# First attention of a two-block transformer kernel: mask and maximum in one VectorE instruction, row sums divided out by diagonal matrices on TensorE, w_ada blocks moved under the rotations

## The reference

```python
# differential head
s1 = q1 @ k1.T * scale;  s2 = q2 @ k2.T * scale        # 256 x 256, causal, 128-query blocks
p1 = softmax(where(mask, s1, -inf));  p2 = softmax(where(mask, s2, -inf))
out = (p1 - lam * p2) @ v
# indexed sparse head: the 64 keys per query with the highest index score, shared by the eight heads
score = sum_h iw[t, h] * relu(iq[t, h] . ik[s]);  sel = top_k(score, 64)
out = softmax(where(valid, q @ k_sel.T * scale, -inf)) @ v_sel
# modulation of the block, from the conditioning vector
mod = silu(c) @ w_ada + b_ada                          # w_ada is 2048 x 12288
```

## Time and profile before

| what | us |
|---|---|
| median of 3 runs | 2853.45 (2843.34 to 2854.09) |
| the profiled execution's own time | 2851.65 |
| its span, first to last instruction | 2849.9 |
| rotations | 354 to 383 |
| index scores | 388 to 410 |
| heads of the first attention | 411 to 491 |

### The profile page before, as it was taken

One profiled execution on the slowest core, in us unless ns is written; L12 is line 12 of the kernel. 1 busy time (PEld: TensorE's weight loads), 2 busy tenths in 40 slices (PEclk: granted clock), 3 DMA queues, 4 the chain that ended last, 5 costly groups with the idle time before them and its releaser, 6 DMA issues. The chain is left out here.

```text
span 2849.9 us, 48016 instructions
## 1 busy us (share of the span) xinstructions
PE 2627.3 (92%) x20028; PEld 2396.6 (84%) x20028; DVE 1424.9 (50%) x1857; ACT 1047.5 (37%) x1335; POOL 268.4 (9%) x324
## 2 busy tenths in 40 slices
PE   5999977969999999999879979798899999999998
PEld 3888834959999999999859947348899999999998
DVE  2455577856674444343353354524555555554443
ACT  3533225334334343333233325323244444443333
POOL 4000030230000000011122000101200000000000
PEclk8999999989999999999989979768999999999999
DMA  7777747745776555555535411002455555554553
GB/s 281 258 247 275 266 146 278 280 138 185 260 271 210 181 189 178 166 190 185 177 89 177 147 37 60 30 0 97 149 169 177 178 178 189 177 182 159 189 182 112
DMA packets 260588, 501.54 MB, mean 176 GB/s; under 512 B 16160, under 2 KB 23035, under 8 KB 260219
## 3 DMA queue, kind: packets, MB, share of 16 engines
q1 hardware_dynamic: 249888, 492.99, 51.5%
q10 hardware_dynamic: 10603, 7.18, 0.9%
HBM read 498.05 MB, written 2.10 MB: 175 GB/s over the span
## 5 line engine op out<-in xcount | busy, mean ns | idle before, releaser
L1127 DVE TENSOR_TENSOR w_lo<-raw,w_hi 128x2048 fp32r<-128x2048 f32 (+2 forms) x386 | 861.1, 2231 | 1079.0 <-ACT w_hi L735 1078.9
L1657 PE MATMUL bank<-x_hi,w_hi 128*128 128x256 f32 (+3 forms) x4608 | 1313.0, 285 | 54.2 <-DVE w_lo L1127 19.2
L1658 PE MATMUL bank<-x_lo,w_hi 128*128 128x256 f32 (+3 forms) x4608 | 1309.8, 284 | 0.0
L1659 PE MATMUL bank<-x_hi,w_lo 128*128 128x256 f32 (+3 forms) x4608 | 1307.8, 284 | 0.0
L735 ACT ACTIVATE w_hi<-raw 128x2048 fp32r<-128x2048 f32 (+2 forms) x386 | 719.1, 1864 | 1075.6 <-PE bank L1659 925.1
L1657 PEld LDWEIGHTS bank<-x_hi,w_hi 128*128 128x128 f32 (+1 forms) x4608 | 875.5, 190 | 90.3 <-issue 40.5
L1659 PEld LDWEIGHTS bank<-x_hi,w_lo 128*128 128x128 f32 (+1 forms) x4608 | 876.6, 190 | 0.0
L1658 PEld LDWEIGHTS bank<-x_lo,w_hi 128*128 128x128 f32 (+1 forms) x4608 | 872.6, 189 | 0.0
L1657 PE MATMUL bank<-hid_hi,w_hi 128*128 128x256 f32 x1408 | 400.0, 284 | 7.9 <-POOL hid_lo L646 6.6
L1658 PE MATMUL bank<-hid_lo,w_hi 128*128 128x256 f32 x1408 | 399.0, 283 | 0.0
L1659 PE MATMUL bank<-hid_hi,w_lo 128*128 128x256 f32 x1408 | 398.9, 283 | 0.0
(11 more groups left out here) (259 smaller groups left out, 1547.3 us busy)
## 6 DMA issues: line engine op xcount, KB each, us to landing
raw<-in_w_ada SPq DMA_DIRECT2D x88, 1024.0 KB, 5.3
raw<-in_w_gate SPq DMA_DIRECT2D x88, 1024.0 KB, 5.2
raw<-in_w_up SPq DMA_DIRECT2D x88, 1024.0 KB, 5.2
raw<-in_w_in SPq DMA_DIRECT2D x68, 1024.0 KB, 5.5
raw<-in_w_down SPq DMA_DIRECT2D x64, 1024.0 KB, 5.1
raw<-in_w_down SPq DMA_DIRECT2D x32, 768.0 KB, 4.3
raw<-in_w_o SPq DMA_DIRECT2D x16, 1024.0 KB, 6.5
raw<-in_w_out SPq DMA_DIRECT2D x16, 1024.0 KB, 5.1
```

The costliest lines, as they stand in the source:

```text
L1127: dve.tensor_tensor(w_lo[ps][:, 0:width], raw[slot][:, 0:width], w_hi[ps][:, 0:width], ALU.subtract).then_inc(raw_free[slot], 1)
L1657: pe.matmul(out, wh[:, k, c], hi(k0 + k), start=a0, stop=False)
L1658: pe.matmul(out, wh[:, k, c], lo(k0 + k), start=False, stop=False)
L1659: ins = pe.matmul(out, wl_[:, k, c], hi(k0 + k), start=False, stop=z)
```

## The change

What it does:

- For heads 0 to 15, `mask` is one `tensor_tensor_reduce` per segment: (scores + bias) times -scale, written to the sheet, with the minimum (the negated maximum) as its accumulated output. The exponential takes scale -1.
- `normalise` only inverts the row sums. GpSimd makes diagonal matrices `diag` (identity times inverse row sum, for sheet 1 also times -lambda), four per differential head and two per dsa head (`diagonals`). `turn` multiplies each sheet block with its matrix, both sheets accumulating in the bank, in place of the transposes.
- The turned dsa sheet is copied by VectorE (`take_turned`) instead of ScalarE.
- Blocks 10 and 11 of w_ada go under the rotations, 12 and 13 between the index scores, 14 to 16 between the heads, one quarter per head and the columns after each fifth head.
- `scores(g)` no longer waits for `h_exp` for g below 26; `exps(g)` also waits for `h_normed` of head g - 2, which GpSimd now sets.

```diff
@@ -267,6 +267,7 @@
         pool_note = place("pool_note", [1, 8])
         gpad_at = cursor[0]
         gpad = place("gpad", [P, 4, NC])
+        diag = place("diag", [P, 2, 4, P], at=gpad_at)
         rope2 = place("rope2", [64, 2, N2], at=gpad_at)
         turns2 = place("turns2", [64, N2], at=gpad_at + 8 * N2)
         acc_at = cursor[0]
@@ -342,6 +343,7 @@
                 i_scored, i_relu, i_added, selected = (sem("index_scored"), sem("index_relu"), sem("index_added"),
                                                sem("selected"))
+        h_inverse = sem("head_inverse")
         h_scored, h_masked, h_exp, h_normed, h_turned, h_copied, h_out, h_taken, h_low = (
             sem("head_" + s) for s in ("scored", "masked", "exp", "normed", "turned", "copied", "out", "taken", "low"))
         m_query, m_scored, m_masked, m_exp, m_normed, m_turned, m_copied, m_out, m_taken = (
@@ -685,6 +687,22 @@
                 pool.wait_ge(bank_freed, BLOCKS_IN1 * 4 + 4)
                 pool.wait_ge(rope_ready, 4)
             rotate_cos("one", projected1)
+
+            def diagonals(g):
+
+                s = g % 2
+                pool.wait_ge(h_inverse, g + 1)
+                if g >= 2:
+                    pool.wait_ge(h_turned, g - 1)
+                for j in range(4 if kind(g) == "diff" else 2):
+                    inv = total[:, s, j:j + 1]
+                    if j < 2:
+                        ins = pool.tensor_scalar(diag[:, s, j, :], ident, inv, None, ALU.mult)
+                    else:
+                        ins = pool.tensor_scalar(diag[:, s, j, :], ident, inv, lamv[:, 5:6], ALU.mult, ALU.mult)
+                ins.then_inc(h_normed, 1)
+            for g in range(16):
+                diagonals(g)
             pool.wait_ge(tile_done, 4 + 4 * BLOCKS_IN1 + 1)
             presum_start("attn_post")
             presum_blocks("attn_post", branch_a, BLOCKS_IN1)
@@ -885,18 +903,24 @@
                     act.activation(lamv[:, 2:4], lamv[:, 0:2], ACT.Exp).then_inc(lam_exp, 1)
                     sines(0, [rope1[:, k, :] for k in range(4)])
 
+            for s in (ADA_HEADS, ADA_HEADS + 1):
+                take_row(s)
+                take_columns(s)
+
             for h in range(16):
                 act.wait_ge(i_scored, h + 1)
                 if h >= 2:
                     act.wait_ge(i_added, h - 1)
                 act.activation(relu[:, h % 2, :], bank[h % 4][:, 0:3 * P], ACT.Relu).then_inc(i_relu, 1)
                 if h in (3, 11):
-                    take_row(ADA_HEADS + h // 8)
+                    take_row(ADA_HEADS + 2 + h // 8)
                 elif h in (7, 15):
-                    take_columns(ADA_HEADS + h // 8)
+                    take_columns(ADA_HEADS + 2 + h // 8)
 
             def exps(g):
                 act.wait_ge(h_masked, g + 1)
+                if 2 <= g < 18:
+                    act.wait_ge(h_normed, g - 1)
                 s = g % 2
                 n = SEGS[kind(g)]
                 for j, (sheet, c0, c1) in enumerate(n):
@@ -907,11 +931,13 @@
                     else:
                         sh = (sheets if g < 16 else sheets2)[:, g % 3, sheet, c0:c1]
                         ins = act.activation(sh, sh, ACT.Exp, bias=peak[:, s, j:j + 1],
-                                             accum_out=total[:, s, j:j + 1])
+                                             scale=-1.0 if g < 16 else 1.0, accum_out=total[:, s, j:j + 1])
                 ins.then_inc(h_exp, 1)
 
             def copy_turned(g):
                 s = g % 2
+                if kind(g) == "dsa":
+                    return
                 act.wait_ge(h_turned, g + 1)
                 if g >= 2:
                     act.wait_ge(h_out, g - 1)
@@ -935,10 +961,10 @@
                 for g in range(g0, g1):
                     if g + 1 < g1:
                         exps(g + 1)
-                    if g < 16 and g % 3 == 2:
-                        take_row(ADA_HEADS + 2 + g // 3)
-                    if g < 16 and g % 3 == 0 and g:
-                        take_columns(ADA_HEADS + 1 + g // 3)
+                    if g < 15 and g % 5 == 4:
+                        take_row(ADA_HEADS + 4 + g // 5)
+                    if g in (5, 10, 15):
+                        take_columns(ADA_HEADS + 3 + g // 5)
                     copy_turned(g)
                     if g > g0:
                         take_out(g - 1)
@@ -1370,13 +1396,15 @@
                     dve.wait_ge(h_turned, g - 2)
                 segs = SEGS[what]
                 sh = (sheets if g < 16 else sheets2)[:, g % 3]
-                if what == "diff":
-                    chain(*[dve.scalar_tensor_tensor(sh[:, m, :], bank[4 * s + m][:, 0:3 * P], QK_SCALE1,
-                                                     causal[:, :], ALU.mult, ALU.add) for m in range(2)])
-                elif what == "dsa":
-                    chain(dve.scalar_tensor_tensor(sh[:, 0, :], bank[4 * s][:, 0:3 * P], DSA_SCALE, selbias[:, :],
-                                                   ALU.mult, ALU.add))
-                elif what == "na":
+                if g < 16:
+                    hidden, scale = (causal, QK_SCALE1) if what == "diff" else (selbias, DSA_SCALE)
+                    for j, (sheet, c0, c1) in enumerate(segs):
+                        ins = dve.tensor_tensor_reduce(sh[:, sheet, c0:c1], bank[4 * s + sheet][:, c0:c1],
+                                                       hidden[:, c0:c1], -scale, -NEG, ALU.add, ALU.min,
+                                                       peak[:, s, j:j + 1])
+                    ins.then_inc(h_masked, 1)
+                    return
+                if what == "na":
                     links = []
                     for b in range(2):
                         rows = bias_na[:, h, 2 - 2 * b:6 - 2 * b, :].rearrange("p r c -> p (r c)")
@@ -1397,19 +1425,23 @@
                 segs = SEGS[what]
                 sh = (sheets if g < 16 else sheets2)[:, g % 3]
                 tot = total[:, s]
+                if g < 16:
+                    dve.reciprocal(tot[:, 0:len(segs)], tot[:, 0:len(segs)]).then_inc(h_inverse, 1)
+                    return
                 chain(dve.reciprocal(tot[:, 0:len(segs)], tot[:, 0:len(segs)]))
-                if what == "diff":
-                    chain(dve.tensor_scalar(tot[:, 2:4], tot[:, 2:4], lamv[:, 5:6], None, ALU.mult),
-                          *[dve.tensor_scalar(sh[:, 0, c0:c1], sh[:, 0, c0:c1], tot[:, j:j + 1], None, ALU.mult)
-                            for j, (_, c0, c1) in enumerate(segs[0:2])])
-                    for j, (_, c0, c1) in enumerate(segs[0:2]):
-                        ins = dve.scalar_tensor_tensor(sh[:, 0, c0:c1], sh[:, 1, c0:c1], tot[:, 2 + j:3 + j],
-                                                       sh[:, 0, c0:c1], ALU.mult, ALU.add)
-                else:
-                    for j, (sheet, c0, c1) in enumerate(segs):
-                        ins = dve.tensor_scalar(sh[:, sheet, c0:c1], sh[:, sheet, c0:c1], tot[:, j:j + 1], None,
-                                                ALU.mult)
+                for j, (sheet, c0, c1) in enumerate(segs):
+                    ins = dve.tensor_scalar(sh[:, sheet, c0:c1], sh[:, sheet, c0:c1], tot[:, j:j + 1], None,
+                                            ALU.mult)
                 ins.then_inc(h_normed, 1)
+
+            def take_turned(g):
+                if kind(g) != "dsa":
+                    return
+                s = g % 2
+                dve.wait_ge(h_copied, g)
+                dve.wait_ge(h_turned, g + 1)
+                dve.wait_ge(h_out, g - 1)
+                dve.tensor_copy(turned[:, s, 0:3 * P], bank[4 * s + 2][:, 0:3 * P]).then_inc(h_copied, 1)
 
             def take_low(g):
                 if kind(g) != "dsa":
@@ -1427,8 +1459,11 @@
                     normalise(g)
                     if g < 7:
                         topk_beside(g)
+                    if g > g0:
+                        take_turned(g - 1)
                     if g > g0 + 1:
                         take_low(g - 2)
+                take_turned(g1 - 1)
                 take_low(g1 - 2)
                 take_low(g1 - 1)
             heads(0, 16)
@@ -1822,6 +1857,10 @@
                         ins = pe.matmul(out, idn, flat(rope_at(rope_buf(which, 1, src), r, src)), start=False,
                                         stop=True)
                     ins.then_inc(r_sum, 1)
+                    if which == "one" and j % 8 in (1, 2, 3, 4) and j < 16:
+                        ada_quarter(ADA_HEADS + j // 8, j % 8 - 1)
+                    elif which == "one" and j % 8 == 7:
+                        ada_columns(ADA_HEADS + j // 8)
             rotate("one")
 
             def turn_values(first, tiles, meta):
@@ -1851,16 +1890,17 @@
                 pe.matmul(b[:, 0:P], q[:, 0:P], ikk[r, 0:P], start=True, stop=True)
```

(20 more changed lines are left out.)

## The result

The changed kernel took 2830.58 us (median of 8 runs, 2828.05 to 2839.73) beside 2852.45 of before (8 runs); the ratio is 0.9933, 95% interval 0.9917 to 0.9950.

A forecast was written before the change was run, and what follows sets the result against it. VectorE was taken to bound the differential heads and TensorE the dsa heads. Differential heads -9.6, dsa heads -1.0 and rotations +1.4 gave -9.2 us, from 2853.45 to 2844 us, with 2834 to 2855 as the 8-in-10 range.

The forecast's parts named there:

- the sum: Whole kernel: differential heads -9.6, dsa heads -1.0 and rotations +1.4 make -9.2 us.
- M = 2.0: VectorE's mask in a differential head: four fused instructions and four readouts take 2.0 us, bounds 1.4 to 3.0.
- The period of 4.1: Differential heads: one head takes 4.1 us after the change, from the loop between the engines.
- my own ring: Differential heads: scores, mask, reciprocal, matrices, turn, outputs, quarter and hand-overs form a loop of two periods, 4.1 us each.
- D = 2.0: GpSimd's four matrices of a differential head, at 0.6 and 0.35 us each with hand-overs: 2.0 us, bounds 1.3 to 2.7.
- The rivals about GpSimd: Heads: GpSimd becomes the bound, 2849 us (chance 0.13); GpSimd is shut out while VectorE works, 2893 us (chance 0.04).
- the second one: Differential heads: GpSimd becomes the bound, 0.85 us per matrix, 3.4 per head, period 4.8, time 2849 us; chance 0.13.
- The half clock at the first turn: Differential heads: first turn, quarter and scores of head 3 run at half clock, making VectorE wait some 2 us.
- dsa heads -1.0: dsa heads: TensorE's work per head becomes 3.56 us, the eight together 31.5 instead of 32.5, so -1.0 us.
- Rotations +1.4: Rotations: quarters cost nothing at full clock, but the first meets a low clock, so +1.4 us (0.3 to 4).
- The median lies 1.8 above it: 2853.45 - 9.2: Whole kernel: the median lies 1.8 us above the profiled execution, so 2853.45 less 9.2 gives 2844 us.
- Only VectorE's work counts: Rival: readouts overlap, matrices take 1.3, TensorE keeps its clock; differential heads -13.5, dsa -2, rotations +0.5: 2838.5 us; chance 0.20.

The follow-up runs named there:

- e8: The changed kernel with the first two diagonal matrices of every head made twice on GpSimd, with a hand-over between; 2847.9 us.
- e10: The changed kernel with dsa heads the old way (normalised on VectorE, transposed, copied on ScalarE); 2835.6 us, turn of head 7 to turn of head 15 25.57.
- e5: The kernel before with only the relaxed wait (scores of heads 2 to 25 no longer wait for the exponentials); 2847.4 us.
- e1: The kernel before with only the fused mask (exponential with scale -1); 2840.9 us.
- e2: The kernel before with only the w_ada blocks moved; 2852.4 us.
- e13: The kernel before with the fused mask and the moved w_ada blocks, without the matrices; 2841.0 us.
- e12: The kernel before with eight tiny chained VectorE instructions ahead of the statistics of the second attention's last heads; 2844.2 us.
- e7: The changed kernel with eight tiny chained VectorE instructions ahead of the statistics of the second attention's last heads; 2830.6 us.
- e11: The changed kernel with dsa heads the old way and the w_ada quarters two rotation steps later; 2825.5 us.
- e14: A repeat of e11, the changed kernel with dsa heads the old way and later w_ada quarters; 2828.8 us.
- e9: The changed kernel with the eight w_ada quarters under rotation steps 3 to 6 and 10 to 13, columns after steps 9 and 16; 2832.4 us.
- e4: The changed kernel with the wait of the scores for the exponentials put back for heads 2 to 25; 2836.6 us.
- e3: The changed kernel with the w_ada blocks back where they were before; 2844.4 us.

## Why the prediction was wrong

The number was off by 13.4 us (2844 and 2830.6), and the heads are not where it was lost: there the sum said -9.2 and the traces have -9.55. From one profiled execution to the other the forecast was -9.2, and they differ by 20.7. What is missing is 3.3 us between `out1` and 644 and 8 us in the long stretch at half clock, both behind the part that the forecast walked through; it put all of that at nothing. Two steps failed, the level of the runs (the bullet on the median; it put the time outside the range) and the price of the mask (the first bullet; the sum hides it).

- **The mask, M = 2.0, bounds 1.4 to 3.0: the step of the mechanism that failed.** It is 1.12. The fused instruction's price was right (0.28 and 0.42 forecast, 0.285 and 0.421 measured), and the readout's too (0.08). Wrong was "I take 2.0, near the upper end, since a readout has to wait for what it reads": its row stands beside that of the next instruction and holds nothing up. The bound of 1.4 was too high as well: "overlapped" still charged the readouts in part. By the rule of the Trainium skill, VectorE: DVE Perf Modes (Rules for kernel authors), not to fuse for speed, the mask would gain nothing here; the measured one, seven instructions to eight and 2.30 us to 1.12, speaks against counting instructions in this case.
- **The period of 4.1 was right for a wrong reason.** By my own ring with M = 1.12 it would be (0.76 + 1.12 + 0.15 + 2.05 + 1.44 + 0.75 + 0.99 + 0.4) / 2 = 3.8. The period is 4.05 because TensorE's own work is 4.05, where I had 3.7: turn 1.44 for 1.3, quarter 0.99 for 0.88, scores 0.87 for 0.76. Two errors, in M and in TensorE's sum, cancelled in the period and not at the start: the reciprocal of head 0 came 3.13 after the first mask in place of 4.3. Differential heads -11.45 for -9.6.
- **D = 2.0** was right: 2.05, of 0.600 and 0.441 for 0.6 and 0.35. The rivals about GpSimd were rightly held unlikely. e8 made the case of the second one real, D of about 3.4: it said 41.8 us from the first mask to the turn of head 7, and 40.04 were measured.
- **The half clock at the first turn** was right: the clock was 0.50 from 417.6 to 424.4, TensorE's scores came late and VectorE waited 4.41 us once, where I had 2.
- **dsa heads -1.0:** to the last copy 32.96 became 32.76, -0.2. A head takes 3.64 for 3.56, and 0.4 more comes behind the last turn. C of e10, 2.42 us shorter, shows that the old turn was the better one here.
- **Rotations +1.4, with "nothing" for a quarter at full clock:** +2.5. A step with a quarter takes 2.05 us, not 1.68, since a pair of rotation matmuls occupies 1.06 and a quarter 0.99, back to back:

```profile
360.45 1.06 PE L1727 MATMUL bank<-raw,csilu 128*32 128x512 f32 x8
361.44 1.12 PE L1853 MATMUL bank<-rope_s,cst 128*128 128x512 f32 x2
362.50 1.06 PE L1727 MATMUL bank<-raw,csilu 128*32 128x512 f32 x8
```

  I had 0.86 + 0.88 = 1.74 from rows of other shapes and wrote off 0.1 a step.
- **The sum, -9.2,** was near what the profile has at the end of the heads, -9.55, by luck: the differential heads gained 1.85 more than forecast, the rotations and dsa heads 1.9 less. Of the -9.55, 0.45 was there before the rotations began (353.33 and 353.78).
- **"The median lies 1.8 above it: 2853.45 - 9.2", with "The second attention's shorter wait: 0" for all that comes behind:** the step that put the time outside the range. The three runs shown, 2843.34, 2853.45 and 2854.09, were two groups, and I took them for one number with a spread. With the forecast's -9.2 the groups stand at 2833 and 2844; the changed kernel falls mostly in the lower, and with the measured -11.5 that group stands at 2830.8. The range had to reach there. "Only VectorE's work counts" (0.20, 2838.5) had the readouts right. It was wrong on the matrices (2.05 for its 1.3), on the clock, which fell to 0.50 at the first turn, and on the total.
- Of the chances, 0.23 for faster by over 0.5% met the result, with the ratio at 0.9933, but not by the rival that carried most of it.

What stays open: why the changed kernel falls in the lower group in 18 of 24 runs and before in 34 of 105. Neither the relaxed wait (e5: 6 of 12), nor the mask (e1: 3 of 10), nor the blocks (e2: 4 of 12), nor mask and blocks together (e13: 3 of 8) do it; a shift may (e12). The matrices were never run by themselves. Most kernels with them have high shares (18 of 24 in the changed kernel, 9 of 10 in e7, 11 of 11 in e11 and e14, 4 of 6 in e9, 7 of 12 in e4), but e8 has them too and 5 of 12, and e3 and e10 have no clear groups. So about half of the distance between the medians has no cause that is shown.

## What to carry to other kernels

When an instruction's tail (a readout, a semaphore) is priced, ask whether the next one of the engine can run beside it, and let the lower bound be the sum of the others from start to start without it (here 2 x (0.22 + 0.34) = 1.12). After a bound is lifted, add up the next engine's rows from start to start at the shapes of the new code, before any loop through several engines. And when the times shown fall apart into groups, forecast for each group, with the share of each as a chance of its own.

## What the runs showed of the hardware

- The accumulator's readout on VectorE takes 0.083 us and adds no time in a row of fused instructions. These take 285 ns for 128 and 421 ns for 256 columns out of a bank, with starts 0.22 and 0.34 apart.
- On GpSimd one multiplication by a column takes 0.600 us for 128 columns and two take 0.441: the shorter instruction does more.
- Under the rotations GpSimd set the pace of 1.68 a step, not VectorE as I had it: GpSimd's products run back to back in before, four in 6.75 us, while VectorE's sum and product of a step, where nothing holds them up, start 0.61 and 0.60 apart (380.77, 381.38 and 381.98 in the changed kernel), 1.21 a step. Beside GpSimd's products VectorE's product with two SBUF inputs takes 1.15 us, and 0.68 where it starts ahead of GpSimd's in the quarter steps of the changed kernel:

```profile
360.69 6.75 POOL L675 TENSOR_TENSOR rope_c<-proj,rope 128x512 f32<-128x512 f32 x4
...
363.48 1.15 DVE L1312 TENSOR_TENSOR rope_s<-proj,rope 128x512 f32<-128x512 f32 x1
```

```profile
363.21 0.68 DVE L1338 TENSOR_TENSOR rope_s<-proj,rope 128x512 f32<-128x512 f32 x1
...
363.37 1.64 POOL L677 TENSOR_TENSOR rope_c<-proj,rope 128x512 f32<-128x512 f32 x1 [0.40 <-DVE proj L1330]
```

- The stretch at half clock in the last heads of the second attention has one of three lengths in these traces, 68.2, 51.2 or 44.3 us (44.4), in code that is the same but for one wait, and in e7 and e12 the shift ahead of it. In e12 another one met the index scores (clock 0.70 from 391 to 413) and cost A 5.4 us.
